# Expert loop in 512-column steps, low parts written over the weight ring, six places for high parts, gate folded into the SwiGLU product

## The reference, cut to what matters

```python
def swiglu(h, w1, w3, w2):
    return (jax.nn.silu(h @ w1) * (h @ w3)) @ w2

def moe(h, router, w1, w3, w2):
    logits = (h @ router).astype(jnp.float32)
    top_v, top_i = lax.top_k(logits, TOP_K)          # TOP_K = 2 of 8
    gates = jax.nn.softmax(top_v, axis=-1)
    dense_gate = jnp.sum(jax.nn.one_hot(top_i, N_EXPERTS, dtype=jnp.float32) * gates[..., None], axis=-2)
    out = jnp.zeros_like(h)
    for e in range(N_EXPERTS):
        out = out + dense_gate[..., e:e + 1].astype(h.dtype) * swiglu(h, w1[e], w3[e], w2[e])
    return out
```

## Time and profile before

| | |
|---|---|
| Median of three runs | 1886.13 us |
| Profiled execution | 1889.37 us |
| its span, first to last instruction | 1887.3 us |
| Mean granted TensorE clock | 0.961 of full speed |
| PE busy | 1794.3 us (95%) |
| DVE busy | 1135.3 us (60%) |
| ACT busy | 944.6 us (50%) |
| HBM read | 384.78 MB, 207 GB/s over the span |

### The profile page before, as it was taken

The page is one execution under the profiler, slowest core; times in us unless marked ns, Lnnn a source line. Parts: engine busy times, 40 slices in busy tenths (PEclk is TensorE's granted clock), DMA queues, the critical chain, the costliest instruction groups (busy, mean ns, idle before and its releaser), DMA issues.

```text
span 1887.3 us, 32736 instructions
## 1 busy us (share of the span) xinstructions
PE 1794.3 (95%) x13637; PEld 1588.9 (84%) x13637; DVE 1135.3 (60%) x1294; ACT 944.6 (50%) x1073; POOL 56.0 (3%) x106
## 2 busy tenths in 40 slices
PE   7999899999999999999889999999999999999995
PEld 6779778899998788868778988898989988898893
DVE  5167124455543155315347878787887878787884
ACT  2444433444332144333336757676766767665672
POOL 3000200010000000020000000000000000000000
PEclk9999799999999999879879999999999999999998
DMA  8124342245457124334177979898997989899860
GB/s 197 61 93 143 131 122 92 71 160 168 154 158 175 56 85 135 123 108 156 34 253 273 365 261 365 271 365 290 333 364 260 363 276 365 288 333 347 276 215 26
DMA packets 350355, 392.22 MB, mean 208 GB/s; under 512 B 24652, under 2 KB 324840, under 8 KB 350264
## 3 DMA queue, kind: packets, MB, share of 16 engines
q1 hardware_dynamic: 345328, 381.05, 61.3%
q0 software_dynamic: 4640, 9.76, 1.4%
q10 hardware_dynamic: 296, 0.07, 0.0%
HBM read 384.78 MB, written 6.08 MB: 207 GB/s over the span
## 4 chain that ended last, share of the span: by engine, by line
PE 90%; ACT 4%; DVE 3%; issue 1%; DMA 1%; POOL 0%; DVEq 0%; ACTq 0%; SPq 0%
PE ps L593 88%; ACT ring L1088 1%; DVE w_lo L1874 1%; PE ps L1012 1%; ACT w_hi L1088 1%; ACT L1088 1%; ACT kvw_hi L1088 1%; DVE ring L1730 1%; DVE dw_lo L1439 0%; ACT low L1088 0%; PE ps L1062 0%; DMA ring<-in_ffd_w_dram 0%; DMA ring<-in_x_sample_dram 0%; DVE att L1737 0%; DVE ring L1748 0%
## 5 line engine op out<-in xcount | busy, mean ns | idle before, releaser
L1874 DVE TENSOR_TENSOR w_lo<-ring,w_hi 128x2048 fp32r<-128x2048 f32 x264 | 603.5, 2291 | 86.6 <-ACT w_hi L1088 79.2
L1088 ACT ACTIVATE w_hi<-ring 128x2048 fp32r<-128x2048 f32 x264 | 504.7, 1913 | 139.4 <-PE ps L593 138.7
L593 PE MATMUL ps<-w_hi,hg_hi 128*96 128x256 f32 x1408 | 398.6, 283 | 2.1 <-DVE hg_lo L1851 2.1
L593 PE MATMUL ps<-w_hi,hg_lo 128*96 128x256 f32 x1408 | 394.7, 280 | 0.0
L593 PE MATMUL ps<-w_lo,hg_hi 128*96 128x256 f32 x1408 | 394.2, 280 | 0.0
L593 PEld LDWEIGHTS ps<-w_hi,hg_hi 128*96 128x96 f32 x1408 | 228.5, 162 | 8.7 <-issue 2.3
L593 PEld LDWEIGHTS ps<-w_lo,hg_hi 128*96 128x96 f32 x1408 | 227.8, 162 | 5.6
L593 PEld LDWEIGHTS ps<-w_hi,hg_lo 128*96 128x96 f32 x1408 | 229.0, 163 | 0.0
L1439 DVE TENSOR_TENSOR dw_lo<-ring,dw_hi 128x2048 fp32r<-128x2048 f32 (+1 forms) x54 | 113.1, 2094 | 113.8 <-ACT dw_hi L1088 113.8
L1088 ACT ACTIVATE low<-ps 96x256 f32<-96x256 f32 (+6 forms) x170 | 66.2, 396 | 190.3 <-PE ps L593 179.5
L1088 ACT ACTIVATE dw_hi<-ring 128x2048 fp32r<-128x2048 f32 (+1 forms) x54 | 94.6, 1752 | 102.5 <-PE ps L593 68.5
(11 more groups left out here) (276 smaller groups left out, 2786.7 us busy)
## 6 DMA issues: line engine op xcount, KB each, us to landing
ring<-in_moe_w_dram SPq DMA_DIRECT2D x264, 1024.0 KB, 5.7
ring<-in_ffd_w_dram SPq DMA_DIRECT2D x22, 1024.0 KB, 5.2
ring<-in_ffd_w_dram SPq DMA_DIRECT2D x16, 704.0 KB, 4.6
ring<-in_w_in_dram SPq DMA_DIRECT2D x14, 768.0 KB, 4.3
ring<-in_w_in_dram SPq DMA_DIRECT2D x8, 1024.0 KB, 5.8
ring<-in_xa_wk_dram SPq DMA_DIRECT2D x8, 1024.0 KB, 5.6
ring<-in_xa_wv_dram SPq DMA_DIRECT2D x8, 1024.0 KB, 5.3
ring<-in_xa_wq_dram SPq DMA_DIRECT2D x8, 1024.0 KB, 5.2
```

The lines of the kernel that those rows point to most:

```text
L593: return nc.tensor.matmul(out, lhsT, rhs, start=first, stop=last)
L1088: return nc.scalar.activation(out, in_, func, **kw)
L1874: V.tensor_tensor(view(w_lo, off, SLOT), view(ring, moe_slot(u) * SLOT, SLOT), view(w_hi, off, SLOT).bitcast(F32), ALU.subtract).then_inc( ...
```

## The change: what it does

- **Steps of 512 hidden columns.** Five steps of 512 and one of 256 take the place of eleven of 256 (`WIDE`, `WSTEPS`). A w1 or w3 unit is now half of the contraction (512 rows) by 512 columns, so `up` is 24 matmuls of 512 columns per weight and step, w1 and w3 in banks of their own. Their order is the table `MOE_PLAN`; there are still 33 units.
- **Low parts over the ring.** `weight_lo` writes the low part over the unit itself. A ring slot is free only once PE has used the unit (`load` now waits on `w_used`).
- **Six places for high parts**, where high and low had three each. `HI_SLOT[u]` is unit u's place, `HI_PREV[u]` the unit that held it before. Units 0 to 17 use six places, 18 to 32 five of them. `HI_PREV[u]` is u - 6 for units 5 to 22 except unit 5 itself (whose place has been free since unit 17 of the expert before), and u - 5 for 0 to 4 and 23 to 32. Five units (`HI_FIRST`), not three, are split ahead of an expert.
- **Orders by rule.** ACT and DVE walk over the units; `after(r)` names what comes behind PE's use of unit r. ACT runs it behind the `weight_hi` that waited for r, DVE ahead of the `weight_lo` that does.
- **Gate in the product.** `multiply` becomes one `scalar_tensor_tensor` (times gate, times silu) that overwrites `sil`. The gate is gathered by three small matmuls at the end of `gather`, and copied by DVE in `gather_lo`.
- **Output split, scatter in float32r.** `scale_y` goes. ACT copies the output to `y_hi`, DVE makes `y_lo`, and a scatter is two float32r matmuls for each of eight results. It is run in two halves: results 0 to 3 behind the first half of w3 of step 0, results 4 to 7 behind the second. PE waits for additions 0 to 5 ahead of w1 of step 1.
- **Order on PE:** down(s - 2), w1 of s, turn(s - 1), w3 of s; at the end down(4), turn(5), gather, down(5).
- Small routing tiles move from `low` to the unused tile `wri`.

With the table's values, DVE's order from the gather on is: gate copy and `gather_lo` (two), low of units 3 and 4, `y_low`, low of 5, 6, 7, additions 0 to 3, low of 8, `multiply(0)`, additions 4 to 7, low of 9, and so on. ACT's is: `gather_hi` (two), high of unit 4 (which waits for PE's use of unit 32, the last), `y_high`, high of 5, 6, 7, `silu(0)`, high of 8, 9, and so on.

```diff
+def moe_plan():
+    ups = [[("w1", s, 0), ("w1", s, 1), ("w3", s, 0), ("w3", s, 1)] if WIDE * (s + 1) <= DFF else
+           [("w1", s, 0), ("w3", s, 0)] for s in range(WSTEPS)]
+    downs = [[("w2", s, j) for j in range(min(2, STEPS - 2 * s))] for s in range(WSTEPS)]
+    order = ups[0] + ups[1]
+    for s in range(1, WSTEPS):
+        order += downs[s - 1] + (ups[s + 1] if s + 1 < WSTEPS else [])
+    return order + downs[WSTEPS - 1]
...
             def load(it, e, u, first=False):
-                kind, s = of_unit[u]
+                key, s, part = MOE_PLAN[u]
                 if u >= RING or not first:
-                    sp.wait_ge(lo_done, it * UNITS_E + u - RING + 1)
+                    sp.wait_ge(w_used, it * UNITS_E + u - RING + 1 + SPLITS)
...
-            def scatter(n):
-                pe.wait_ge(y_scaled, n + 1)
-                for d in range(KD):
+            def scatter(n, d0, d1):
+                if d0 == 0:
+                    pe.wait_ge(y_split, n + 1)
+                for d in range(d0, d1):
                     if d >= 4:
                         pe.wait_ge(scat_added, n * KD + d - 3)
-                    mm(ps[:, 4 + d % 4, 0:T], y_sb[0:C, P * d:P * d + P], selT[0:C, :], True, True).then_inc(scat_ready, 1)
+                    bank = SCAT_BANK[d % 4]
+                    mm(ps[:, bank, 0:T], y_hi[0:C, P * d:P * d + P], selT[0:C, :], True, False)
+                    mm(ps[:, bank, 0:T], y_lo[0:C, P * d:P * d + P], selT[0:C, :], False, True).then_inc(scat_ready, 1)
...
                 pe.wait_ge(hg_ready, it + 1)
-                up(0)
-                scatter(it)
-                up(1)
+                up_all("w1", 0)
+                up("w3", 0, 0)
+                scatter(it, 0, 4)
+                up("w3", 0, 1)
+                scatter(it, 4, KD)
+                pe.wait_ge(scat_added, it * KD + 6)
+                up_all("w1", 1)
                 pe.wait_ge(scat_added, it * KD + KD)
...
                 turn(0)
-                for s in range(2, STEPS):
-                    up(s)
+                up_all("w3", 1)
+                for s in range(2, WSTEPS):
+                    down(s - 2, 0)
+                    down(s - 2, 1)
+                    up_all("w1", s)
                     turn(s - 1)
-                    down(s - 2)
-                turn(STEPS - 1)
+                    up_all("w3", s)
+                down(WSTEPS - 2, 0)
+                down(WSTEPS - 2, 1)
+                turn(WSTEPS - 1)
                 if not last_one:
                     gather(it + 2)
-                down(STEPS - 2)
-                down(STEPS - 1)
+                down(WSTEPS - 1, 0)
...
+            def y_high(n):
+                act.wait_ge(w_used, n * UNITS_E + SPLITS)
+                act.wait_ge(down_zeroed, 1)
+                f(y_hi[0:C, :], ps[0:C, 4:6, :].rearrange("p b n -> p (b n)"), ACT.Copy).then_inc(y_hi_done, 1)
...
-            def scale_y(n):
-                dve.wait_ge(w_used, n * UNITS_E + SPLITS)
-                V.tensor_scalar(y_sb[0:C, :], ps[0:C, 2:4, :].rearrange("p b n -> p (b n)"), gs[0:C, 0:1], None,
-                                ALU.mult).then_inc(y_scaled, 1)
+            def y_low(n):
+                dve.wait_ge(y_hi_done, n + 1)
+                V.tensor_tensor(y_lo[0:C, :], ps[0:C, 4:6, :].rearrange("p b n -> p (b n)"),
+                                y_hi[0:C, :].bitcast(F32), ALU.subtract).then_inc(y_split, 1)
...
-                V.tensor_tensor(view(w_lo, off, SLOT), view(ring, moe_slot(u) * SLOT, SLOT),
-                                view(w_hi, off, SLOT).bitcast(F32), ALU.subtract).then_inc(lo_done, 1)
+                V.tensor_tensor(view(w_lo[moe_slot(u)], 0, SLOT), view(ring, moe_slot(u) * SLOT, SLOT),
+                                view(w_hi, HI_SLOT[u] * SLOT, SLOT).bitcast(F32), ALU.subtract).then_inc(lo_done, 1)
...
+                def after(r):
+                    if r == UNIT_AT["w3", 0, 0]:
+                        add_y(it, 0, 4)
+                    for s in range(WSTEPS):
+                        if r == LAST_UP["w3", s]:
+                            multiply(s)
+                        if s and r == LAST_UP["w1", s]:
+                            act_lo(s - 1)
+                            if s == 1:
+                                next_sel()
+                    if r == UNIT_AT["w3", 0, 1]:
+                        add_y(it, 4, KD)
+                    if r == UNIT_AT["w2", WSTEPS - 2, 1]:
+                        act_lo(WSTEPS - 1)
+                        if not last_one:
+                            gather_lo(it + 2)
+
+                y_low(it)
+                done = -1
+                for u in range(HI_FIRST, UNITS_E + (0 if last_one else HI_FIRST)):
+                    prev = HI_PREV[u] if u < UNITS_E else UNITS_E + HI_PREV[u - UNITS_E]
+                    while done < prev:
+                        done += 1
+                        after(done)
+                    weight_lo(it + u // UNITS_E, u % UNITS_E)
+                for r in range(done + 1, UNITS_E):
+                    after(r)
+
+            for u in range(HI_FIRST):
+                weight_lo(0, u)
             gather_lo(1)
```

More of the change, by code:

```diff
@@ L252, in layer_program @@
         w_hi = over("w_hi", [P, SPLITS * SLOT], at["hT"])
-        w_lo = over("w_lo", [P, SPLITS * SLOT], at["hT"] + 4 * SPLITS * SLOT)
+        w_lo = [over(f"w_lo{i}", [P, SLOT], at["ring"] + 4 * i * SLOT) for i in range(RING)]
         c_mix, c_xa, c_ff, c_mem, c_fin = 0, 16, 32, 48, 64
@@ L990, in _, with parts @@
             gather(1)
             def expert(it, last_one):
-                def parts(kind, s):
-                    u = unit_of(kind, s)
+                def parts(u):
                     pe.wait_ge(lo_done, it * UNITS_E + u + 1)
[L996 to L1005, removed]
+                    return as_unit(w_hi, HI_SLOT[u] * SLOT, u), as_unit(w_lo[moe_slot(u)], 0, u)
@@ new lines, in up @@
+                def up(key, s, part):
+                    u = UNIT_AT[key, s, part]
+                    wh, wl = parts(u)
+                    whole = WIDE * (s + 1) > DFF
+                    width, k0, nk = (DFF - WIDE * s, 0, KD) if whole else (WIDE, KD // 2 * part, KD // 2)
+                    bank = 2 * (s % 2) + (key == "w3")
+                    for k in range(nk):
+                        last_ = split_mm(ps[0:C, bank, 0:width], hg_hi[:, k0 + k, :], hg_lo[:, k0 + k, :],
+                                         wh[:, k, :], wl[:, k, :], k0 + k == 0, k0 + k == KD - 1)
+                    last_.then_inc(w_used, 1)
@@ L1050, in _ @@
             expert(more * NE + (NE - 1), True)
-            scatter(more * NE + NE)
+            scatter(more * NE + NE, 0, KD)
             pe.wait_ge(scat_added, more * (NE * KD) + (NE + 1) * KD)
@@ new lines, in expert @@
+                y_high(it)
+                done = -1
[3 more added lines that the diff above has]
+                        done += 1
+                        if done < prev:
+                            after(done)
+                    weight_hi(it + u // UNITS_E, u % UNITS_E)
+                    after(prev)
+                for r in range(done + 1, UNITS_E):
+                    after(r)
@@ L1409, in _ @@
             expert(more * NE + (NE - 1), True)
+            y_high(more * NE + NE)
             norm(3 * LAYERS, lambda d: act.wait_ge(scat_added, more * (NE * KD) + NE * KD + d + 1))
@@ L1927, in _ @@
             expert(more * NE + (NE - 1), True)
-            scale_y(more * NE + NE)
-            add_y(more * NE + NE)
+            y_low(more * NE + NE)
+            add_y(more * NE + NE, 0, KD)
             norm(3 * LAYERS, c_fin)
```

258 lines of the change are left out of this document (125 added, 133 removed).

## The result

The changed kernel takes **1902.13 us** (median of seven runs, 1899.94 to 1903.54), the kernel before 1886.60 beside it. The ratio is 1.0062 [1.0048, 1.0075]: slower by 0.6%, 15.5 us. The forecast was 1896 us, with 1888 to 1906 for its own case. The profiled execution after took 1902.86 us, its span is 1901.2 (before 1887.3), its mean clock 0.949 (before 0.961).

The account below looks back on a forecast made before the run. PE was taken to pace the expert loop, DVE close behind. Start, stalls, savings and end gave +2.7 us and the clock +7.8 on 1889.37, so 1899.9; less 3.2, 1896 us, range 1872 to 1912.

Parts of the forecast that it names:

- its own case: PE waits for DVE's additions between experts and the clock falls there: 1888 to 1906 us, chance 0.55.
- The stall: PE waits for DVE's additions ahead of w1 of step 1: 5.06 us per expert, until 20.86 after `gather_hi` starts.
- The savings: On PE per expert: wide matmuls 1.10, float32r scatter 1.53, wait at turn(10) 2.01; together 4.64 us less.
- the turn's wait: PE's wait for DVE at turn(10), ahead of the gather: 2.01 us per expert, claimed to go.
- the net: Per expert, 5.06 us of waiting for additions minus 4.64 us saved on PE: 0.42 us more.
- The clock: PE's clock falls: 14.0 us at seven stalls, 2.0 at the first expert, minus 8.2 for earlier falls; +7.8.
- Rival 1: The clock holds at PE's stalls: all 16.0 us go, 1880 us, or 1888 with half of them; chance 0.22.
- rival 2: DVE is not behind, additions 4 and 5 are done by 15.8 after `gather_hi` starts: 1843 us, chance 0.12.
- rival 3: DMA becomes the bound in the expert loop, a step taking 18.0 us: 1938 us, chance 0.04.
- Rival 4: A longer chain or slower clock recovery, 1 us more at each stall and beyond: 1904 us and above, chance 0.07.
- The start: Five low parts on DVE, not two, ahead of the first gather's split: PE starts the first expert 2.0 us later.
- the carry-over: The 3.2 us by which the earlier kernel's median lay below its profiled execution, taken off 1899.9 to give 1896.

Follow-up runs that it names:

- the reordered kernel: Changed kernel with DVE's additions 0 to 3 moved ahead of low(6), 4 to 7 ahead of low(7), multiply(0) ahead of low(8): 1850.18 us, 0.9801 of before.

## Why the prediction was right

- **The stall.** Forecast 5.06 us from + 15.80 to + 20.86; measured + 20.81. The terms without a row held too: `y_hi` 1.02 (taken as 1.04), `y_lo` 1.22 (taken as 1.27), `multiply` 0.66 to the next start (0.66), four additions 1.54 (1.50). In the first expert the wait is 1.83 (1.9).
- **The savings.** Wide matmuls of the up projection start 0.23 us apart, the scatter's half takes 1.06 to the next matmul's start, the turn's wait is gone. Without the stall an expert takes 102.70 us, 4.25 less than 106.95; forecast 4.64. The missing 0.39 is near the small waits that remain even in the reordered kernel, 0.19 for additions and 0.16 for `a_lo` in each expert. The same small waits put w1 of step 1 at + 16.24 there and not at + 15.80, so the stall is worth 4.57, and not 5.06. Both halves of the net were 0.4 to 0.5 too large, and so it came out near: with the clock kept up in the filled stall, two experts are 107.25 apart, 0.30 more than 106.95, where the prediction had 0.42.
- **The clock.** It fell at all seven stalls, at 2.02 us each where it was measured by itself (2.0), and again behind the first gather. Rival 1 falls. The rule of the Trainium skill (TensorE: Matmul & The Clock Gate, "HAM oscillation — how this bites in real kernels") points the same way, and the runs add its limit: with the wait of 3.13 alone, three of seven heads kept the clock. One fall was not forecast, the one behind the first expert's wait of 1.83 us. And the waits of 2.01 us in the kernel before are eight, not seven: the last expert has one too, without a fall, so a wait of that length was enough in five of eight cases.
- **The rivals 2 to 4.** DVE is behind, so rival 2 falls; with three moves in its queue it isn't, and the time, 0.9801 of before, is near the 1843 us put on it (0.977). ACT waits for no load in the expert loop of the changed kernel, and the reordered one runs an expert in 102.70, so rival 3 falls. Rival 4 has no stall longer than counted.
- **What was mis-sized.** From the first matmul of the first expert to the last output the terms gave +8.0 (7 x 0.42 - 2.7 + 14.0 + 2.0 - 8.2), and +8.4 is measured without `y_hi`. That is in part luck: the fall behind the first expert's wait is in the measured time and not in the terms, and it is worth about 1.6 us (the first expert is 2.23 shorter with a wait 0.65 shorter and no fall), so the terms were some 1.2 too high without it. The start gave +2.0, and +1.9 came. The 6 us by which 1902 misses 1896 lie elsewhere. The 3.2 us between profiled execution and median were carried over as clock falls; but the changed kernel has its falls at every head, and its profiled execution is only 0.7 us above its median: 2.5 us. Ahead of the experts 1.5 us came in, with nothing in the change for them, and no more than the executions differ there. At the end +2.0 came (`y_hi` and the 1.0 behind it) where the prediction had +0.5: the sum of squares ran at the slow clock (6.50 us instead of 4.15), which took more than the half scatter gave. The rest is rounding and 0.4 us less around the span. Without the carry-over the sum, 1899.9, lay 2.2 below the median.

## What to carry to other kernels

When a change shortens the engine that paces, write out the queue of its supplier between two iterations with start times, and ask of every small instruction that the pacing engine waits for what stands ahead of it. Here eight additions of 0.4 us behind low parts of 2.2 us that were needed later turned a gain of 2% into a loss of 0.6%, and moving them and one multiplication forward gave all of it back. Price a stall of TensorE twice, by its length and by the clock behind it, and separate the two by filling it. A stall that is only made shorter can pay less than its own length: here 0.65 us off each wait left the middle experts within 0.34 us of their old length, as long as the clock still fell.

## What the runs showed of the hardware

- A fall of the clock does not follow from one wait's length alone. In the kernel before, a wait of 2.01 us was followed by a fall in five of eight cases. In the changed kernel 1.05 and 3.13 us close together were followed by one in six of six, and 0.25 and 3.13 us in the one case there is; with `multiply(0)` moved back, and 2.48 us in place of 3.13, it was again all seven. With high(4) early, 3.13 us alone had a fall behind it in four of seven. In the first expert 1.83 or 1.84 us alone had one in three of three kernels (the changed one and those with low(3) and high(4) early), and 1.18, 0.84 and 0.19 us had none. The stall filled with matmuls had none in seven heads.
- With w1 and w3 loaded in rows of 2 KB instead of 1 KB, all but their last step, the same 381.05 MB went from 345,328 packets to 263,408, and a load of 1024 KB landed 5.1 us behind its issue in the median, against 5.7. The page's list of DMA issues, after:

```profile
ring<-in_moe_w_dram SPq DMA_DIRECT2D x264, 1024.0 KB, 5.1
```

That loads land sooner is no gain of bandwidth by itself: they are also issued by another schedule, and no run here tells the two apart.
